# A mixture-of-experts tail without a final stage: expert blocks keep running sums, norm and store the rows themselves

## The reference, cut to what matters

```
x2 = x1 + sum over the row's two experts e of  w_e * (silu(h2 @ w_gate[e]) * (h2 @ w_up[e])) @ w_down[e]
y  = x2 * rsqrt(mean(x2 * x2) + 1e-6) * norm_final
```

## Time and profile before

| | us |
|---|---|
| median of 3 runs (lowest, highest) | 1054.56 (1053.7, 1055.37) |
| span of the profiled execution | 1050.6 |
| TensorE busy (matmuls) | 1000.8 (95%) |
| VectorE busy | 553.1 (53%) |
| ScalarE busy | 422.6 (40%) |
| GpSimd busy | 89.0 (8%) |
| moved by DMA | 220.95 MB, 210 GB/s over the span |
| chain of waits, TensorE's share | 87% |

### The profile page before, as it was taken

How to read it: one execution, slowest core, us unless ns; L and a number is a source line. 1 busy time by engine, 2 the same in 40 slices (tenths; PEclk the granted TensorE clock), 3 DMA queues, 4 the chain that set the end, 5 groups by cost and what they waited for, 6 DMA issues and landing times.

```text
span 1050.6 us, 17421 instructions
## 1 busy us (share of the span) xinstructions
PE 1000.8 (95%) x6832; PEld 927.5 (88%) x6832; DVE 553.1 (53%) x951; ACT 422.6 (40%) x827; POOL 89.0 (8%) x115
## 2 busy tenths in 40 slices
PE   5999999989999999999999989999999999999954
PEld 4889999989999999998888788999999999999822
DVE  7457767796535445466566573334443343444117
ACT  7487786433233233232232132343343434333115
POOL 2000000000000000000300030111121211211000
PEclk9999999999999999999999999999999999999988
DMA  6114767336744644566312188999898888899357
GB/s 240 44 43 127 160 159 193 107 101 178 208 119 135 189 125 120 151 212 188 105 52 81 45 321 306 387 342 341 322 339 339 319 335 323 342 352 328 119 201 316
DMA packets 118030, 220.95 MB, mean 210 GB/s; under 512 B 68428, under 2 KB 81286, under 8 KB 109262
## 3 DMA queue, kind: packets, MB, share of 16 engines
q1 hardware_dynamic: 105762, 194.20, 55.8%
q0 software_dynamic: 9792, 17.19, 4.3%
q10 hardware_dynamic: 2412, 8.68, 2.1%
HBM read 191.79 MB, written 46.72 MB: 227 GB/s over the span
## 4 chain that ended last, share of the span: by engine, by line
PE 87%; DVE 6%; ACT 3%; DMA 2%; issue 1%; SPq 0%; ACTq 0%; DVEq 0%; POOLq 0%
PE psum L1141 27%; PE psum L2194 23%; PE psum L2045 10%; PE psum L2256 8%; PE psum L2176 3%; PE psum L2219 1%; PE psum L1164 1%; PE psum L1980 1%; DVE it L953 1%; DVE xi L955 1%; PE psum L1246 1%; DMA y<-expert_rows 1%; DVE acc L897 1%; PE psum L1233 1%; PE psum L1239 1%
## 5 line engine op out<-in xcount | busy, mean ns | idle before, releaser
L1141 PE MATMUL psum<-hh,wh 128*128 128x350 f32 x672 | 223.4, 333 | 3.9 <-issue 3.9
L1141 PE MATMUL psum<-hh,wl 128*128 128x350 f32 x672 | 218.0, 324 | 0.0
L1141 PE MATMUL psum<-hl,wh 128*128 128x350 f32 x672 | 217.2, 323 | 0.0
L1141 PEld LDWEIGHTS psum<-hh,wh 128*128 128x128 f32 x672 | 127.8, 190 | 5.3 <-issue 4.1
L1141 PEld LDWEIGHTS psum<-hl,wh 128*128 128x128 f32 x672 | 127.6, 190 | 0.9
L2194 PE MATMUL psum<-xgt,wg 128*128 128x128 f32 x1088 | 127.1, 275 | 0.2 <-ACT xgt L2185 0.2
L1141 PEld LDWEIGHTS psum<-hh,wl 128*128 128x128 f32 x672 | 127.2, 189 | 0.0
L2194 PE MATMUL psum<-xgt,wu 128*128 128x128 f32 x1088 | 127.0, 275 | 0.0
L2194 PEld LDWEIGHTS psum<-xgt,wg 128*128 128x128 f32 x1088 | 124.3, 192 | 0.4 <-issue 0.3
L2194 PEld LDWEIGHTS psum<-xgt,wu 128*128 128x128 f32 x1088 | 124.2, 192 | 0.0
L2235 DVE TENSOR_TENSOR wd_lo<-wd,wd_hi 128x2048 fp32r<-128x2048 f32 x30 | 68.8, 2292 | 86.8 <-ACT wd_hi L2231 86.8
(11 more groups left out here) (336 smaller groups left out, 1573.8 us busy)
## 6 DMA issues: line engine op xcount, KB each, us to landing
wg<-w_gate SPq DMA_DIRECT2D x34, 1024.0 KB, 6.7
wu<-w_up SPq DMA_DIRECT2D x34, 1024.0 KB, 9.3
wd<-w_down SPq DMA_DIRECT2D x34, 1024.0 KB, 13.2
wst<-w_in SPq DMA_DIRECT2D x28, 512.0 KB, 3.7
ck<-qkv_rows SPq DMA_DIRECT2D x9, 702.0 KB
qkv_rows<-acc SPq DMA_DIRECT2D x12, 520.0 KB, 6.1
xb<-x SPq DMA_DIRECT2D x8, 512.0 KB, 4.4
wo<-w_out SPq DMA_DIRECT2D x8, 512.0 KB, 7.0
```

Source lines behind the costliest of these rows:

```text
L1141: ins = mm(ps[:, c, 0:ZC], w[:, kk, :], a[:, kk, c * ZC:(c + 1) * ZC], start=(kk == 0 and q == 0), stop=(kk == KD - 1 and q == 2))
```

## The change

There is no final stage and no table `expert_rows`. Its place is taken by `sum_rows` in HBM, one row for each token. The router part stores x1 into it (9 stores on SyncE). Each block gathers the running sums of its tokens (`gather_sum`), adds its own weighted result to them (`add_rows`, one VectorE instruction over 128 x 1024 that replaces the two halves), and scatters them back (`scatter_sum`). Each block also takes the sum of squares (`square`, ScalarE), the inverse root (`inverse_root`, 12 VectorE instructions over 128 x 1) and scales (`scale`); these three run in the step after, as a fourth stage `behind`. `scatter_y` writes y for the rows whose later expert this block is; the table's column 1 is now the token's number there and outside the bounds otherwise (3 more VectorE instructions for each router tile, 6 for the further blocks). Two experts of a group share tokens, so a block must not gather sums before the last block of its group has scattered them: the blocks take the four groups in turn (`expert_of`), and a group comes again four blocks later. GpSimd issues four indirect DMAs for each block in place of two. In the further blocks the order is transposes and gate/up of the first, transposes of the second, down of the first, gate/up and down of the second.

```diff
@@ router
+            step(tt(second, ms2, ms, ALU.is_lt))
+            step(tt(vals[:, 1, 1, t:t + 1], vals[:, 0, 1, t:t + 1], second, ALU.mult))
+            step(tt(vals[:, 1, 0, t:t + 1], vals[:, 0, 0, t:t + 1], vals[:, 1, 1, t:t + 1], ALU.subtract))
...
+    def residual_stored(sp, t):
+        n = rows(t)
+        sp.dma_start(b.sum_d[t * P:t * P + n, :], b.x1[0:n, t, :]).then_inc(b.x1_out, 16)
@@ experts
+def expert_of(block):
+    return EPG * (block % GRP) + block // GRP
...
+    def gather_sum(pool, q, p, e):
+        pool.indirect_dma_start(before[p][:, :], None, b.sum_d, rows_of(0, e), bounds_check=TOK - 1, oob_is_err=False
+                                ).then_inc(q.sum_in.sem, 16)
+    def scatter_sum(pool, q, p, n, e):
+        pool.wait_ge(q.sum_ok.sem, q.sum_ok.at(n + 1))
+        pool.indirect_dma_start(b.sum_d, rows_of(0, e), total[p][:, :], None, bounds_check=TOK - 1, oob_is_err=False
+                                ).then_inc(q.sum_out.sem, 16)
+    def scatter_y(pool, q, p, n, e):
+        pool.wait_ge(q.y_ok.sem, q.y_ok.at(n + 1))
+        pool.indirect_dma_start(io.y, rows_of(1, e), y[p][:, :], None, bounds_check=TOK - 1, oob_is_err=False
+                                ).then_inc(q.y_out.sem, 16)
...
-    def weigh_a(act, q, p, n, e):
-    def weigh_b(dve, q, p, n, e):
+    def add_rows(dve, q, p, n, e):
+        dve.wait_ge(q.down_ok.sem, q.down_ok.at(n + 1))
+        dve.wait_ge(q.sum_in.sem, q.sum_in.at(16 * (n + 1)))
         if later(n):
+            dve.wait_ge(q.sum_out.sem, q.sum_out.at(16 * n))
+        nc.vector.scalar_tensor_tensor(
+            total[p][:, :].rearrange("c (h d) -> c h d", h=2), ps[0:C, 4 + 2 * p:6 + 2 * p, :], weight(e),
+            before[p][:, :].rearrange("c (h d) -> c h d", h=2), ALU.mult, ALU.add).then_inc(q.sum_ok.sem, 1)
+    def square(act, q, p, n):
+        act.wait_ge(q.sum_ok.sem, q.sum_ok.at(n + 1))
         if later(n):
+            act.wait_ge(q.y_out.sem, q.y_out.at(16 * n))
+        nc.scalar.activation(y[p][:, :], total[p][:, :], ACT.Square, accum_out=roots[p][:, 0:1]
+                             ).then_inc(q.squared.sem, 1)
+    def inverse_root(dve, q, p, n):
...
+        step(nc.vector.tensor_scalar(v, ss, 1.0 / D, EPS, ALU.mult, ALU.add))
+        step(nc.vector.tensor_scalar(half_bits[p][:, 0:1], v.bitcast(I32), 1, None, ALU.logical_shift_right))
+        step(nc.vector.tensor_scalar(guess, half_bits[p][:, 0:1], -1.0, float(0x5f3759df), ALU.mult, ALU.add))
+        for k in range(3):
+            step(nc.vector.scalar_tensor_tensor(t, at, at, v, ALU.mult, ALU.mult))
+            step(nc.vector.tensor_scalar(h, t, -0.5, 1.5, ALU.mult, ALU.add))
+            step(nc.vector.tensor_tensor(to, at, h, ALU.mult))
+    def scale(dve, q, p, n):
+        nc.vector.scalar_tensor_tensor(y[p][:, :], total[p][:, :], roots[p][:, 6:7], wn[:, :], ALU.mult, ALU.mult
+                                       ).then_inc(q.y_ok.sem, 1)
@@ staggered, in the loop (the same before and after it)
                 front(block_of(j + 2, i))
+                behind(block_of(j + 3, i - 1))
                 mid(block_of(j + 1, i))
                 back(block_of(j, i))
@@ SyncE, after the first four experts
+            sp.wait_ge(b.x1_out, 16 * TILES)
+            sp.dma_start(wn[:, :], io.norm_final.partition_broadcast(P)).then_inc(wn_in.sem, 16)
@@ GpSimd
+            pool.wait_ge(b.x1_out, 16 * TILES)
+            for e in range(2):
+                gather_sum(pool, main[e], e, expert_of(e))
             for e in range(NE):
...
                 if e < NE - 2:
                     pool.wait_ge(x.q.turned.sem, x.q.turned.at(x.n + 1))
                 if e + 4 < NE:
-                    gather(pool, b, x.k, e + 4)
+                    gather(pool, b, x.k, expert_of(e + 4))
...
-                scatter(pool, x.q, x.p, x.n, e)
+                pool.wait_ge(x.q.sum_ok.sem, x.q.sum_ok.at(x.n + 1))
+                if e + 2 < NE:
+                    if x.n > 0:
+                        pool.wait_ge(x.q.sum_out.sem, x.q.sum_out.at(16 * x.n))
+                    gather_sum(pool, x.q, x.p, expert_of(e + 2))
+                scatter_sum(pool, x.q, x.p, x.n, expert_of(e))
+                scatter_y(pool, x.q, x.p, x.n, expert_of(e))
@@ VectorE
+            def behind(x):
+                if isinstance(x.e, int) and x.e == 0:
+                    dve.wait_ge(wn_in.sem, wn_in.at(16))
+                norm(dve, x.q, x.p, x.n)
-            staggered(dve, nothing, mid, lambda x: weigh_b(dve, x.q, x.p, x.n, x.e))
+            staggered(dve, nothing, mid, lambda x: add_rows(dve, x.q, x.p, x.n, x.id), behind)
@@ removed: final_parts(...), all_scattered(...), and their calls
```

More of the change, by code:

```diff
@@ L1565, in route_parts @@
         r[name] = m.place("r_" + name, [P, k])
-    one = m.place("r_one", [P, 8])
-    mg, ms, m1, m2, d, sg, ed, den = (one[:, k:k + 1] for k in range(8))
+    one = m.place("r_one", [P, 10])
+    mg, ms, m1, m2, d, sg, ed, den, ms2, second = (one[:, k:k + 1] for k in range(10))
     lx = m.place("r_lx", [P, GRP, EPG])
@@ L2135, in expert_stage @@
     assert m.at <= b.C
+    m.at = b.R1
+    wn = m.place("wn", [C, D])
+    before = [m.place(f"before{k}", [C, D]) for k in range(2)]
+    y = [m.place(f"y{k}", [C, D]) for k in range(2)]
+    roots = [m.place(f"roots{k}", [C, 8]) for k in range(2)]
+    half_bits = [m.place(f"half_bits{k}", [C, 2], I32) for k in range(2)]
+    assert m.at <= b.R1 + 8 * 4 * D
+    wn_in = s.again("wn_in")
     m.at = b.he_at
@@ new lines, in expert_stage @@
+    ends = dict(turned=blocks, xt_ok=2 * blocks, gu_ok=blocks, tanh_ok=blocks, ge_ok=blocks, he_ok=blocks,
+                down_ok=blocks, sum_ok=blocks, squared=blocks, root=ROOT * blocks, y_ok=blocks,
+                sum_in=16 * blocks, sum_out=16 * blocks, y_out=16 * blocks)
+    qm = {n: [Again(q[n][p].sem, q[n][p].ended + ends[n]) for p in range(2)] for n in names + landed}
+    more = [StepSems({n: qm[n][p] for n in names + landed}) for p in range(2)]
+    more_w, more_gathered = s.again_pair("v_w"), [Again(b.gathered[p], 16 * NE // 4) for p in range(2)]
@@ L2315, in further @@
         return count
-    def all_scattered(eng, count):
-        for p in range(2):
-            eng.wait_ge(main[p].scattered.sem, main[p].scattered.at(16 * (NE // 2)))
-        for n in range(OV // 2):
-            with eng.If_lt(eng.to_reg(2 * n), count):
-                for p in range(2):
-                    eng.wait_ge(more[p].scattered.sem, more[p].scattered.at(16 * (n + 1)))
     def nothing(x):
         pass
-    final = final_parts(nc, m, s, b, io)
     stages = front
@@ L2352, in _ @@
             sp.wait_ge(b.ove_ok.sem, b.ove_ok.at(1))
-            count = further(sp, body)
-            all_scattered(sp, count)
-            final.weights(sp)
-            final.loads(sp)
+            further(sp, body)
             sp.wait_ge(b.state_out, 16)
```

245 lines of the change are left out of this document (82 added, 163 removed).

## The result

The kernel after takes 1071.99 us (median of 4 runs, 1067.64 to 1073.42), the kernel before 1054.68 beside it (4 runs): ratio 1.0151 [1.0129, 1.0172]. It is 1.5% slower; the forecast was 1042, and the range ended at 1064. The profiled run took 1073.42, its span 1071.7.

What follows compares the result with a forecast made beforehand. TensorE, busy without a gap in the expert stage, was taken as the bound, transfers close behind. 1050.6 - 21.4 (end) + 0.6 (router) + 3.5 (start) + 5 (gather stall) = 1038.3 of span; the median lies 4.0 higher: 1042, range 1028 to 1064.

Steps and rivals of the forecast that it cites:

- the DMA system's: Expert stage: transfers rise from some 338 to 373 GB/s, 10.8 us of a 10.84 us step, and just fit.
- 5 were taken: Expert stage: h2's gather stalls TensorE some 0.6 us in one step of four, 5 us in all.
- (9.7 + landing)/2: Expert stage: step length when h2's gather, issued 9.7 us into the step behind `scatter_y`, lands late; 11.85 at landing 14.
- rival 2: Expert stage, h2's gather behind `scatter_y`: GpSimd's queue fills; slower above a mean landing of 13.2 us, 1067 at 14; chance 0.25.
- A longer step also relieves the DMA: Expert stage: longer steps hold the gather's stall down; at a step of 11.4 the DMA share is back near 0.95.
- The start: First blocks: the first norm waits for norm_final's row, so block 5's gather is late; 3.5 us, ends 0 and 8.
- The router: Router part: three more one-column instructions on the last tile's chain cost 0.6 us; the rest is covered.
- The end: After the last main down product: without the final stage the kernel ends at 1029.2, 21.4 us below 1050.6.
- root instructions: Norm in each step: 12 one-column VectorE instructions for the inverse root, taken at 0.24 us each, 2.9 us.
- VectorE's order: Expert step: w_down's low part moves behind the scaling, from S+3.8 to S+7.5 (S: step's start); 7 us remain, nothing paid.
- TensorE's waits at the semaphore of `xg`: Expert stage, expected sign: gaps before the transposes put down to h2's gather DMA, 0.5 us and more a step if slower.
- nothing at the additions: Expert stage: running sums' scatters and gathers have room; stalls at the additions' semaphores would show the prediction wrong.

## Why the prediction was wrong

**The step that failed is the DMA system's: "So the rate is close to full, by one count at 99%, by the other at 93%, and just fits."** The amounts were right: 3.5 passes for 2, demand 373 GB/s, share 10.8 us of 10.84. The ceiling was not. It was read from a window of 6 us at 401 GB/s and a share of 1.00; the kernel after sustains 346 GB/s at 0.91 with its mix of weights and rows. The 50 us window beside it, 372 at 0.95, did not last either: the kernel after has such a stretch (358 at 0.95, 700 to 750), four steps of 10.8, and then falls to 335 to 348, probably when what was loaded ahead is used up. By the line 11.85 us a step against 10.83: 25.5 us over the 25 steps where 5 were taken; measured 26.6. (The line was drawn after the fact and is no prediction.)

**The mechanism of the stall, "(9.7 + landing)/2", described it and did not cause it.** With the gather issued at S + 11.7, a landing of 13.0 and the transposes at S + 1.3 it gives 11.7, near the measured 11.89; rival 2, "GpSimd's queue fills", was so the nearest case, with its chance of 0.25, and its place and its sign came true. That its 1067 lies near the 1072 is partly luck: it went with a landing of 14, and at the measured 13.0 it gave no change to speak of; what made up for it was the issue, 2.0 us later than taken. The place itself, h2's gather behind `scatter_y`, does not decide, as the run with the gather moved ahead showed: the landing stretched from 13.0 to 20.1 and the step stayed. "A longer step also relieves the DMA" was right as a thought and wrong in its number: the share came back not to 0.95 at steps of 11.4, but to 0.91 at 11.9.

**The start: 3.5 us taken, 5.3 measured.** From the issue of the last load ahead of it (653.8) to the landing of the norm's row (669.0) 15.2 us went by, for 11.3 taken; VectorE waited 10.8 us, and steps 4 and 5 lost 6.9 us against before. Here the rate was not at fault: from 656 to 669 us the window shows 376 GB/s at a share of 0.99, so 4.9 MB, where the sum counted 3.7. It left out what other DMAs moved meanwhile.

```profile
656.00:669.00 13.00, 13.00 (x91) 10.60 (x90) 1.28 (x1) 4.30 (x6) 2.01 (x2) 1.00 0.99 376
```

With the row loaded early, the gain was partly given back by the later steps.

**The router: 0.6 us taken.** The runs can't tell: equal code reaches block 0 up to 9 us apart in the profiled executions, and 3.4 of the 7.0 us belong to the mixer, at a lower granted clock.

**The end: right in its parts, 2.9 us short.** -18.5 for -21.4. Block 31's addition waited for the landing of block 29's sum, issued at 1008.57 and 14.00 us under way (9.0 taken); the idle time before the further blocks' first product was 6.9 us (7 taken), and that product ran 8.94 for 7.16 of the next, 1.8 (1.7 taken). The last `scatter_y` is issued at 1062.16, and the span ends 9.5 us later; 4.6 were taken for its landing and GpSimd's closing.

**What held:** root instructions 0.21 us each; VectorE's order (the norm ahead of w_down's low part pays nothing in a step); TensorE's waits at the semaphore of `xg`; nothing at the additions.

## What to carry to other kernels

Before adding transfers to a stage, take its sustained rate from a long stretch in which the compute engine waits for transfers of the same mix. While it does not wait, a window's rate is the demand, and the 401 GB/s of 6 us were not to be had for long here. If no such stretch exists, make one: cut some compute out and see where the step stops falling, which costs one run and here would have said 0.55 us of room, where the prediction itself counted 1.0 us of new packets. When a wait names a queue, check by swapping orders whether the landing stretches by as much as the issue moved; if so, the order is not the lever, what is moved is. And before an experiment is read as showing a ceiling, look into its chain for a wait that its own edit put there.

## What the runs showed of the hardware

- **A sustained rate that falls as row gathers and scatters are added:** 381 GB/s or more at one pass, 355 at two, 345 to 348 at three, 340 to 347 at 3.5, 333 at four (there perhaps by the loop through `out`), at DMA shares from 0.98 down to 0.87. The Trainium skill (DMA: Bandwidth & Descriptors, "Where 436 GB/s comes from") gives some 435 GB/s for the fabric and some 358 for HBM per core, and says that for transfers between HBM and SBUF the second binds. The rates here lie below it from two passes on, and above it at one: at 381 GB/s it did not bind.
- **Slots out of bounds cost nearly nothing:** two indirect scatters a block with all slots skipped lengthened a step from 10.83 to 10.87 us.
- **An indirect DMA instruction on GpSimd takes 2.25 to 2.41 us in place of 1.01 beside VectorE's subtraction of two SBUF tiles.** With the scatter of the kernel before put beside it, the steps stayed at 10.83.
- **The size of the other queue's packets sets GpSimd's landings:** 7.7 us beside gate and up loads of 4 KB rows, 13.0 beside 8 KB rows, at nearly the same step (12.04 and 11.89). This agrees with the rule of the Trainium skill (DMA: Bandwidth & Descriptors, "Queues, rings and completion order") that each DMA engine takes turns by packets, which the prediction cites; what GpSimd's queue gained, w_down lost (24.7 us for 16.7).
